# A two-block transformer layer stack on one core: evictions, scans and weight splits re-ordered in the hybrid mixer; index flips, causal mask and query norm moved in the sparse mixer

## What is computed

```python
def hybrid_mixer(h, w_in, conv_w, ...):
    z, xbc, dt_raw, qm, km, vm, om, ig, fg = split_cols(h @ w_in, HY_SPLITS)
    xbc = silu(causal_dwconv(xbc, conv_w, conv_b))           # xs, B, C
    dt = softplus(dt_raw + dt_bias); A = -exp(a_log)
    y = ssd_chunked(xs, dt, A, B, C, 128)                    # needs cumsum(dt * A), exp of it
    y = rms_norm((y + xs * d_skip) * silu(z))
    hm = mlstm_chunked(qm, km, vm, ig, fg, 128)              # needs cumsum and running max of the gates
    return concat([y, rms_norm(hm) * sigmoid(om)]) @ w_out

def sparse_attention(h, cos, sin, w_in, q_norm, k_norm, w_out, topk=64):
    q, k, v, qi, ki, wi = split_cols(h @ w_in, SA_SPLITS)    # 16 q heads, 1 k, 1 v, 8 index heads
    q = rope(rms_norm(q, q_norm)); k = rope(rms_norm(k, k_norm)); qi, ki = rope(qi), rope(ki)
    score = sum_h(relu(qi_h @ ki.T) * wi_h) * scale
    score = where(causal, score, -inf)
    sel = top_k(score, topk)                                 # per query, shared by all heads
    s = where(selected and causal, q_h @ k.T / 8, -inf)
    return concat_h(softmax(s) @ v) @ w_out
```

## Time and profile before

| | us |
|---|---|
| median of 3 executions (2467.55 to 2475.57) | 2467.65 |
| the profiled execution | 2469.09 |
| its span in the trace | 2467.3 |
| PE busy | 2433.5 (99%) |
| DVE busy | 1788.2 (72%) |
| ACT busy | 1127.4 (46%) |
| DMA, mean | 166 GB/s |
| mean granted TensorE clock | 0.987 |

### The profile page before, as it was taken

How to read it: one execution, slowest core, us unless ns; L and a number is a source line. 1 busy time by engine, 2 the same in 40 slices (tenths; PEclk the granted TensorE clock), 3 DMA queues, 4 the chain that set the end, 5 groups by cost and what they waited for, 6 DMA issues and landing times.

```text
span 2467.3 us, 39959 instructions
## 1 busy us (share of the span) xinstructions
PE 2433.5 (99%) x16787; PEld 2231.3 (90%) x16787; DVE 1788.2 (72%) x2169; ACT 1127.4 (46%) x1310; POOL 66.1 (3%) x94
## 2 busy tenths in 40 slices
PE   8999999999999999999999999999999999999999
PEld 7999799899999968999999988999999999899998
DVE  8778655877877767778777676587787767666876
ACT  4335555433433545334334763443343357544332
POOL 2000000000000000100000000001000000000000
PEclk9999999999999979999999999999999999999999
DMA  6555335555555414665554533466555545344554
GB/s 207 185 185 171 111 120 173 186 188 187 179 184 186 130 52 127 210 196 184 188 187 156 171 120 126 149 199 211 189 174 187 186 156 171 111 129 158 184 187 136
DMA packets 308123, 409.43 MB, mean 166 GB/s; under 512 B 9782, under 2 KB 274448, under 8 KB 307984
## 3 DMA queue, kind: packets, MB, share of 16 engines
q1 hardware_dynamic: 304176, 400.61, 50.8%
q0 software_dynamic: 3072, 5.69, 0.8%
q10 hardware_dynamic: 736, 1.13, 0.1%
HBM read 406.35 MB, written 1.05 MB: 165 GB/s over the span
## 4 chain that ended last, share of the span: by engine, by line
PE 95%; DVE 2%; ACT 1%; DMA 1%; issue 0%; ACTq 0%; DVEq 0%
PE acc L585 25%; PE bank L546 24%; PE bank L987 16%; PE bank L549 12%; PE bank L985 2%; PE acc L2111 2%; PE bank L572 1%; PE acc L546 1%; PE bank L565 1%; PE bank L2635 1%; PE acc L2128 1%; PE bank L1783 1%; PE acc L2229 1%; PE acc L549 1%; PE bank L2083 1%; DVE part_lo L479 1%
## 5 line engine op out<-in xcount | busy, mean ns | idle before, releaser
L472 ACT ACTIVATE part_hi<-raw 128x2048 fp32r<-128x2048 f32 x383 | 728.5, 1906 | 923.6 <-DMA raw<-in_ffn_w 383.4
L479 DVE TENSOR_TENSOR part_lo<-raw,part_hi 128x2048 fp32r<-128x2048 f32 x383 | 870.6, 2277 | 246.9 <-ACT part_hi L472 244.4
L546 PE MATMUL bank<-hT,part_hi 128*128 128x512 f32 x2560 | 641.6, 392 | 0.0
L546 PEld LDWEIGHTS bank<-hT,part_hi 128*128 128x128 f32 x2560 | 460.9, 189 | 83.0
L585 PE MATMUL acc<-gated,part_hi 128*128 128x256 f32 x2816 | 519.9, 283 | 0.0
L585 PEld LDWEIGHTS acc<-gated,part_hi 128*128 128x128 f32 x2816 | 445.1, 192 | 0.0
L987 PE MATMUL bank<-part_hi,hT 128*128 128x256 f32 (+1 forms) x2336 | 440.0, 288 | 0.2
L585 PE MATMUL acc<-gated,part_lo 128*128 128x256 f32 x1408 | 398.5, 283 | 0.0
L987 PEld LDWEIGHTS bank<-part_hi,hT 128*128 128x128 f32 x2336 | 372.7, 194 | 6.1 <-issue 4.3
L549 PEld LDWEIGHTS bank<-hT,part_lo 128*128 128x128 f32 x2560 | 349.2, 190 | 24.9
L549 PE MATMUL bank<-hT,part_lo 128*128 128x256 f32 x2560 | 356.9, 282 | 0.0
(11 more groups left out here) (441 smaller groups left out, 2260.0 us busy)
## 6 DMA issues: line engine op xcount, KB each, us to landing
raw<-in_ffn_w SPq DMA_DIRECT2D x132, 1024.0 KB, 5.3
raw<-in_w_in SPq DMA_DIRECT2D x52, 1024.0 KB, 5.3
raw<-in_ffn_w_gate SPq DMA_DIRECT2D x44, 1024.0 KB, 5.3
raw<-in_ffn_w_up SPq DMA_DIRECT2D x44, 1024.0 KB, 5.3
raw<-in_ffn_w_down SPq DMA_DIRECT2D x44, 1024.0 KB, 5.0
raw<-in_hy_w_in SPq DMA_DIRECT2D x22, 1024.0 KB, 5.3
raw<-in_hy_w_out SPq DMA_DIRECT2D x8, 1024.0 KB, 4.9
raw<-in_w_out SPq DMA_DIRECT2D x8, 1024.0 KB, 4.9
```

The source lines that it names most:

```text
L472: t.e.activation(part_hi[:, n % SLOTS, 0:size], raw[:, n % SLOTS, 0:size], ACT.Copy).then_inc(hi_ready, 1)
L479: t.e.tensor_tensor(part_lo[:, n % SLOTS, 0:size], raw[:, n % SLOTS, 0:size], part_hi[:, n % SLOTS, 0:size].bitcast(F32), ALU.subtract).th ...
L546: pe.matmul(b.rearrange("p (h s) -> p h s", h=2), slot_cols(s, 0)[:, k, f * P:(f + 1) * P], hT[:, :, k, :], start=(k == 0), stop=False, sk ...
```

## The change

Hybrid mixer: the SiLU of B and C moves on ACT to between the fifth and the sixth tap. V1 and V2 are evicted without the `next_hi` ahead of them, which follows after other work; the two Exp of the decays go ahead of the last `next_hi` and V3's eviction. On DVE a `next_lo` ahead of the fifth convolution goes; one stays before the scans and one follows them.

Sparse mixer: PE projects P0 to P3, flips the index queries and keys, and then P4. The causal mask (0 or 1 in `sa_bias`, times -1e30 on the diagonal of `sa_ident`) is added to the index sum by a matmul, so that top-k reads `acc` at once; the final bias is one operation. P6 comes after the flips of k and of q heads 0 to 3; the flips of heads 4 to 7 are in step 1 of the loop. The root of the query norm is no longer multiplied into q (the two L1975 go): it is the scale of the Exp, and DVE multiplies it into the row maximum of each head (one 128x2 operation). The Exp table is loaded early by a dummy operation. DVE's remaining splits go to steps 7, 8, 8, 12, 12, ACT's to 8, 8, 12, 16. The last output piece starts with the k tile of heads 12 and 13.

Cut to its core:

```diff
@@ hybrid_scalar
+                if i == 4:
+                    act.wait_ge(hy_conv, 2)
+                    silu_of(8, 12).then_inc(hy_bc, 1)
...
             project_scalar(t, mvs[0:1])
-            act.wait_ge(hy_conv, 2)
-            silu_of(8, 12).then_inc(hy_bc, 1)
             act.wait_ge(hy_conv, 4)
             silu_of(0, 4).then_inc(hy_xs, 1)
-            project_scalar(t, mvs[1:2])
-            act.wait_ge(hy_conv, 6)
-            silu_of(4, 8).then_inc(hy_xs, 1)
+            v_out(mvs[1])
             b = filled(t)
...
-            project_scalar(t, mvs[2:3])
+            act.wait_ge(hy_conv, 6)
+            silu_of(4, 8).then_inc(hy_xs, 1)
+            next_hi(t)
+            v_out(mvs[2])
+            next_hi(t)
...
-            project_scalar(t, mvs[3:4])
             act.wait_ge(hy_decay_in, 1)
...
+            project_scalar(t, mvs[3:4])
@@ hybrid_vector
-            project_vector(t, 1)
             conv_of(4)
...
             conv_of(5)
             project_vector(t, 1)
+            t.banks.take(by_piece=True)
...
             dve.sem_inc(hy_decay_in, 1)
+            next_lo(t)
@@ index_tensor
-            all_taken(t)
@@ sparse_tensor
-            project_tensor(t, SA_W[0:5], h_waits=hT_waits(t), root=True)
-            flip_tensor(t, lambda k, a: sa[:, a, SA_QI + k * P:SA_QI + (k + 1) * P], 4)
-            flip_tensor(t, lambda k, a: sa_kd[:, a, 1, :], 1)
+            project_tensor(t, SA_W[0:4], h_waits=hT_waits(t), root=True)
+            index_in = flip_tensor(t, lambda k, a: sa[:, a, SA_QI + k * P:SA_QI + (k + 1) * P], 4)
+            index_in += flip_tensor(t, lambda k, a: sa_kd[:, a, 1, :], 1)
+            project_tensor(t, SA_W[4:5])
+            for evicted_at in index_in:
+                pe.wait_ge(*evicted_at)
             made = index_tensor(t, 0) + index_tensor(t, 4)
...
+            pe.matmul(acc[:, 2, 0:SA_ROW], sa_ident[:, :], sa_bias[:, :], start=True, stop=False, skip_group_check=True)
...
-            project_tensor(t, SA_W[5:7])
-            flip_tensor(t, lambda k, a: sa_kd[:, a, 0, :], 1)
-            flip_tensor(t, lambda k, a: sa[:, a, k * P:(k + 1) * P], 4)
-            all_taken(t)
+            project_tensor(t, SA_W[5:6])
+            heads_in_flips = flip_tensor(t, lambda k, a: sa_kd[:, a, 0, :], 1)
+            heads_in_flips += flip_tensor(t, lambda k, a: sa[:, a, k * P:(k + 1) * P], 2)
+            project_tensor(t, SA_W[6:7])
+            for evicted_at in heads_in_flips:
+                pe.wait_ge(*evicted_at)
             pe.wait_ge(sa_mask, 1)
...
+                if i == 1:
+                    second_flips = flip_tensor(t, lambda k, a: sa[:, a, (k + 2) * P:(k + 3) * P], 2)
+                if i == 2:
+                    pe.wait_ge(*last_piece)
...
-            pe.wait_ge(sa_out_lo, SA_H)
-            out_rows_tensor(t, 6)
+            pe.wait_ge(sa_out_lo, SA_H - 2)
+            out_rows_tail(t)
@@ sparse_scalar
-            project_scalar(t, tiles[0:1])
-            root_row_scalar(t)
-            project_scalar(t, tiles[1:3])
...
+            next_hi(t)
+            out_of(0)
+            root_row_scalar(t)
+            next_hi(t)
+            out_of(1)
+            written = out_of(2)
+            next_hi(t)
+            act.wait_ge(*written)
...
+            diagonals(0)
+            first = out_of(3)
             flip_scaled_scalar(t, sa_qiT, 4)
             flip_scaled_scalar(t, sa_kiT, 1)
+            diagonals(1).then_inc(sa_diag_made, 1)
...
+            next_hi(t)
+            second = out_of(4)
...
             index_scalar(t, 0)
             index_scalar(t, 4)
-            project_scalar(t, tiles[5:7])
+            next_hi(t)
+            act.activation(gated_room[:, 0:1], ident[:, 0:1], ACT.Exp)
+            third = out_of(5)
...
-                                             bias=sa_m[:, i % 2, 0, a:a + 1], accum_out=sa_m[:, i % 2, 1, a:a + 1])
+                                             bias=sa_m[:, i % 2, 0, a:a + 1], scale=head_root(i)[:, a:a + 1],
+                                             accum_out=sa_m[:, i % 2, 1, a:a + 1])
@@ sparse_vector
-            dve.tensor_copy(sa_ident[:, :], ident)
+            dve.tensor_scalar(sa_ident[:, :], ident, NEG, None, ALU.mult)
+            for a, o, n in SA_PARTS:
+                dve.tensor_scalar(sa_bias[:, o:o + n], late(C_CAUS + a * S, n), 0.0, None, ALU.is_lt)
...
-            project_vector(t, 3)
+            project_vector(t, 2)
+            t.banks.take(by_piece=True)
...
-            rooted(0)
-            turn(first, 8, gained)
+            turn(first, 8, gained, some=slice(0, 4))
+            next_lo(t)
+            next_lo(t)
...
+            turn(first, 8, gained, some=slice(4, 8))
...
-            for a, o, n in SA_PARTS:
-                ins = dve.tensor_tensor(sa_sc[:, o:o + n], acc[:, 2, o:o + n], late(C_CAUS + a * S, n), ALU.add)
-            t.link(ins)
-            for _ in range(TOPK // 8):
+            for turn_n in range(TOPK // 8):
+                rest = acc[:, 2, :] if turn_n == 0 else sa_sc
...
-            t.link(dve.tensor_scalar(sa_sc[:, :], sa_sc[:, :], 0.5 * TAKEN_KEY, NEG, ALU.is_gt, ALU.mult))
             for a, o, n in SA_PARTS:
-                ins = dve.tensor_tensor(sa_bias[:, o:o + n], sa_sc[:, o:o + n], late(C_CAUS + a * S, n), ALU.add)
+                ins = dve.scalar_tensor_tensor(sa_bias[:, o:o + n], sa_sc[:, o:o + n], 0.5 * TAKEN_KEY,
+                                               sa_bias[:, o:o + n].bitcast(F32), ALU.is_gt, ALU.max)
...
-                    ins.then_inc(sa_max, 1)
+                    t.link(ins)
+                    dve.tensor_tensor(sa_m[:, i % 2, 0, :], sa_m[:, i % 2, 0, :], head_root(i), ALU.mult).then_inc(sa_max, 1)
...
-                if i == 3:
-                    rooted(8)
-                if i == 4:
-                    turn(second, 8, gained)
-                if i == 5:
+                if i == 3:
+                    root_vector(t, stat[:, 0, 16:32], 64)
+                if i in (4, 5):
+                    turn(second, 8, gained, ((0, 1), (2, 3))[i - 4])
+                if i == 6:
                     joined(second, 8)
```

More of the change, by code:

```diff
@@ L892, in flip_tensor @@
         def flip_tensor(t, src, n, rows_out=P, order=None):
-            pe = t.e
+            pe, out = t.e, []
             pe.wait_ge(flip_src, t.see(flip_src))
@@ L896, in flip_tensor @@
                 b = claim(t)
+                out.append((taken[b], t.banks.uses[b]))
                 for k in range(k0, min(k0 + 2, n)):
@@ L901, in flip_tensor @@
                 mm.then_inc(full[b], 1)
+            return out
         def flip_out(t, dst, n, scale, rows_out, mine):
@@ L1344, in hybrid_scalar, with v_out @@
                         .then_inc(hy_gate_log, 1)
+                if i == 4:
+                    act.wait_ge(hy_conv, 2)
+                    silu_of(8, 12).then_inc(hy_bc, 1)
             mvs = [mv[:, :, i, 0:ML_V] for i in range(4)]
+            def v_out(dst):
+                b = t.banks.take(by_piece=True)
+                act.wait_ge(piece_done, SLOTS + t.piece + 1)
+                for a in range(TT):
+                    ins = act.activation(dst[:, a, :], halves(b)[:, a, :], ACT.Copy, scale=root_col[:, a:a + 1])
+                ins.then_inc(taken[b], 1)
             project_scalar(t, mvs[0:1])
-            act.wait_ge(hy_conv, 2)
-            silu_of(8, 12).then_inc(hy_bc, 1)
             act.wait_ge(hy_conv, 4)
             silu_of(0, 4).then_inc(hy_xs, 1)
-            project_scalar(t, mvs[1:2])
-            act.wait_ge(hy_conv, 6)
-            silu_of(4, 8).then_inc(hy_xs, 1)
+            v_out(mvs[1])
             b = filled(t)
@@ L1743, in out_rows_tensor, with head_banks, out_rows_tail @@
                                    k == KD - 1)
-                if k0 == KD - 2 and d in (1, 3, 5):
+            mm.then_inc(piece_done, 1)
+        OUT_STEPS = (8, 12, 16)
+        HI_STEPS = (8, 8, 12, 16)
+        LOW_STEPS = (7, 8, 8, 12, 12)
+        def head_banks(t, to_come=0):
+            b = (t.banks.next + to_come - 1) % 4
+            return ((b + 1) % 4, (b + 2) % 4), (b + 3) % 4, b
+        def out_rows_tail(t):
+            pe = t.e
+            s = arrived(t)
+            order = [(d, k) for k in (6, 7) for d in range(4)] + [(d, k) for d in range(4, KD) for k in (6, 7)]
+            for d, k in order:
+                if k == 7 and d == 0:
+                    pe.wait_ge(sa_out_lo, SA_H)
+                mm = down_tile(pe, lambda w: slot_rows(s, w)[:, k - 6, :], lambda g: hT[:, g, k, :], d, False, k == KD - 1)
+                if k == 7 and d in (1, 3, 5):
                     mm.then_inc(acc_full, 1)
             mm.then_inc(piece_done, 1)
-        OUT_STEPS = (8, 12, 16)
-        LOW_STEPS = (7, 9, 11, 13, 14)
         def sparse_tensor(t):
@@ L1846, in sparse_scalar, with out_of @@
             tiles = [sa[:, :, i * COLS:i * COLS + w] for i, w in zip(SA_TILES, SA_W)]
+            n0 = t.piece
```

(40 more changed lines are left out.)

110 lines of the change are left out of this document (56 added, 54 removed).

## The result

The changed kernel takes 2448.18 us (median of 4 runs, 2446.56 to 2449.58), the kernel before 2467.6 beside it (4 runs, 2467.05 to 2475.57): ratio 0.9914, 95% interval 0.9892 to 0.9935, some 19.4 us less. The forecast was 2441.0 with a range of 2434.5 to 2450.0. The time lies in the range, but 7 us above the likeliest case and at rival A's 2447.5, a case up to which the range had been stretched. The profiled execution took 2447.06 (span 2445.2), 22.0 less than the one of before.

A forecast was written before the change was run, and what follows sets the result against it. PE, busy 99% of the span, was taken as the bound. Terms 9.4 + 8.8 + 7.2 + 3.2 - 2.0 = 26.6 us off the profiled 2469.1 gave 2442.5, or 2441.0 as a median; range 2434.5 to 2450.0.

The forecast's parts named there:

- rival A: Sparse head loop: the clock falls at its start and heads 0 to 7 stay at 31 us; 2447.5, chance 0.14.
- Hybrid mixer, 9.4: Hybrid mixer to Q0's end: waits gone, V3 earlier, spreads and Q0 at full clock; 9.4 us gained, all let through.
- Sparse mixer to the loop, 8.8: Sparse mixer before the head loop: earlier index sum, shorter top-k and pause; loop begins 8.8 us earlier.
- tie, to within 1.5 us: Index stage: DVE's added work ends at 851.7, when PE's sum is ready, to within 1.5 us.
- Heads 0 to 7, 7.2: Head loop, first half: DVE, not PE, is the bound; 23.8 us in place of 31.0, 7.2 us gained.
- 2.0 taken off for the clock: Head loop: PE's new pauses in steps 4 and 7 may lower the clock; 2.0 us lost, the middle taken.
- The bad end of 3.5: Head loop: clock falls once near head 4, returns with the late flips; 3 heads slowed, some 3.5 us.
- Heads 8 to 15, 3.2: Head loop, second half: DVE splits moved beneath output pieces and an early last piece; 3.2 us gained from 44.24.
- B: Hybrid mixer: the wait only changes its name, clock falls, decays late again; 3 us gained, not 9.4; 2447.4, chance 0.12.
- C: Both mixers: rival A and B together, and top-k 3 us late behind DVE's deferred work; 2457, chance 0.04.
- D: Head loop: DVE's longer circle keeps the clock at 1.2 GHz through heads 8 to 15 too; slower, 2472, chance 0.02.
- E: Both mixers: the targeted waits go but something else holds PE; 2460, chance 0.03.

The follow-up runs named there:

- the execution without a fall: Changed kernel unaltered, measured a third time, with no fall of the clock in the hybrid mixer: 2444.06 us.
- with filling: Changed kernel with six 128x256 matmuls, or three 128x128 transposes, put in PE's pause ahead of the head loop: 2441.25 and 2441.87 us.
- the filled kernel: Changed kernel with six 128x256 matmuls, on which nothing depends, put in PE's pause ahead of the head loop: 2441.25 us, ratio 0.9898.
- the old sparse code: Only the hybrid mixer's part of the change, on the kernel before: 2462.28 us, ratio 0.9976.
- the kernel with the constant: The filled kernel with Exp's scale set to the constant 1.0 in place of the per-row root: 2440.60 us.
- filling in the heads alone: Changed kernel with three 128x256 matmuls behind the scores of each of heads 0 to 7, nothing ahead of the loop: 2444.05 us.

## Why the forecast was right in its range and 7 us off in its likeliest case

**Hybrid mixer, 9.4.** Right. V3 began at 265.86, less the 0.37 by which this execution was late 265.5, forecast 265.3. The spreads ran at 1.00 and Q0 ended at 281.30, 9.0 us earlier than 289.94 once the 0.37 is taken off. In the execution without a fall the hybrid stretch is 218.56, 9.06 less than before. The mistake is in the sentence "so I let all of it through": eight of the twelve profiles of the new hybrid code have one fall of 3.4 us in the stretch, worth 1.5 us, at 274 to 276 or at 320, three have two or three falls (223 to 226 us), and one has none. PE had no pause between V3 and any of them.

**Sparse mixer to the loop, 8.8.** Measured 8.33 (857.37 - 812.91 against 872.84 - 820.05). PE's sum was done when the forecast said, but DVE was not (PE, then DVE):

```profile
839.18 5.40 PE L1799 MATMUL acc<-sa_index,sa_diag 128*128 128x128 f32 x32
```

```profile
841.39 1.22 DVE L2061 TENSOR_REDUCE stat<-squares 128x16 f32<-128x1024 f32 x1 [0.16 <-DVE sa L2007]
...
844.86 0.17 DVE L860 TENSOR_TENSOR stat<-stat 128x16 f32<-128x16 f32 x1
845.07 0.63 DVE L2077 MAX8 sa_m<-acc 128x8 f32<-128x128 f32 x2
```

The root of the first eight q heads ends at 845.03, and the first pass of top-k follows on it at once; the sum had ended at 844.58. That is the "tie, to within 1.5 us", lost by 0.45, and it is most of why 0.63 us of pause stayed ahead of the loop where the forecast had 0.1.

**Heads 0 to 7, 7.2, with 2.0 taken off for the clock.** Here the likeliest case failed. The 23.8 us were right for a clock of 1.00 (23.91 and 23.93 with filling), and so was DVE as the bound. That they agree to 0.1 us is in part luck: the forecast added 21.5 us of DVE's work and 2.3 of waits, and the trace has 20.26 and 3.65. The step that failed is the clock's price, "it falls once near head 4 and comes back with the late flips, 3 heads", 0 to 3.5 us. The fall came at head 2 in two profiles of three and at head 5 in the third, and it cost 6.2, 6.2 and 1.6 us against 23.91. The 3.9 us that it took for a head at 0.50 was a mean that took in the short first heads; a full one takes 4.50 in both traces. The bad end of 3.5 was too low mainly because it let the first heads off: it looked for pauses of 2 us in steps 4 and 7, and in two profiles of three the clock fell where PE had paused for 0.63 at most. In the third it fell right behind a pause of 1.48 us in step 5, but the filled kernel has the same pause, at 870.74, and no fall. Rival A said "PE's work there is sparse even when its queue is never empty", and that is what the trace shows, in the loop and at 320.65; it should have had far more than 0.14. The evidence against it, that heads 8 to 15 held 1.00 with the same matmuls, was weak. Output pieces stand between those heads, and in four of the later profiles one fall of 3.4 us lies there all the same (at 883, 887, 890 and, with the old sparse code, 930). The page "TensorE: Matmul & The Clock Gate" of the Trainium skill, in "A second HAM failure mode: psum-queue depth-cycling", tells of a kernel in which frequent short idle times between groups of matmuls made the clock swing. This case agrees that no long pause is needed (0.63 us at most ahead of the fall at 860), and goes further, since at 320.65 it fell with no pause at all.

**Heads 8 to 15, 3.2.** Measured 44.24 to 41.63, 2.6. The operand of Exp, which the forecast had not priced, takes 0.7 of it back: from head 8 on the kernel with the constant is 0.7 shorter than the filled one (1.21 for the sparse stretch less 0.48 for heads 0 to 7). With it the splits and the early last piece gave 3.3.

**Sum.** In the sparse stretch the forecast had 8.8 + 7.2 + 3.2 - 2.0 = 17.2. The changed kernel gave 11.75, 11.77 and 16.45 in its three profiles, the filled one 18.11. Of the 5.4 missing in the first, 4.2 are the clock (6.2 for 2.0), 0.5 the way to the loop, 0.6 heads 8 to 15 and 0.1 heads 0 to 7. The hybrid mixer lacks 1.85, 1.5 of it by its fall. So the measured time lies in the range because the range took in rival A, and rival A's fall came in heads 0 to 7 for nearly its full price, not because the forecast's own case did. The other rivals did not come: B's wait stayed at 1.5 us and left the decays on time, C's deferred work held DVE up by 0.45 us, D's clock was 1.00 in heads 8 to 15 of the changed kernel, and E's waits did not turn up elsewhere.

**What stays open.** Why one execution of a kernel keeps the clock to head 5 and the next loses it at head 2, on the same instructions at nearly the same times. Nor do the runs tell whether the pause of 0.63 us has a part in it: the clock fell behind it at head 2, at head 5 and at head 6, and with filling in the heads alone it did not fall behind it. How much room the filling leaves is open too, and whether the kernels with more falls in the hybrid mixer had them by chance.

## What to carry to other kernels

A chain of small matmuls can run at half clock with PE "busy" throughout and stay there, here for 27 us: at 1.2 GHz PE was busy all the time and nothing showed as a wait. So read the granted clock of such a stretch before its waits, price it at both levels, and take the lower level as likely, not as the exception, even after every long wait ahead of it has been removed. Compare single profiles stage by stage with a ruler of common instructions, and count a difference in a stage that the change does not touch (here 3.1 us) as none of its doing; in this kernel falls alone move a run by several us.

## What the runs showed that was not expected

- The clock fell at 320.65 us with PE busy without a gap since 265.86, behind stretches of spreads and matmuls of 64 columns, and on the same instructions it did not fall in another execution. That fall lasted 3.4 us and cost 1.5 us (220.07 against 218.56).
- Three transposes in a pause of 0.63 us, of which 0.2 stayed, went with a clock of 1.00 through eight heads (23.93 us), as six dense matmuls did (23.91); one profile of each.
- An Exp with a per-row scale read from SBUF takes 0.09 to 0.10 us more than with a constant (0.46 and 0.56 against 0.37 and 0.46): 1.2 us over sixteen heads.
- The kernel before varies too: 2464.04 to 2474.04 in 13 runs, a spread of 10 us, more than any single term of the forecast.
